# Experts' gate/up weights in half-chunk transfers, and a round's kind and units from registers

## What is computed

```python
logits = hf @ w_router + b_router               # 32 experts
top_vals, top_idx = lax.top_k(logits, 4)
weights = softmax(top_vals)
# each token's 4 experts:
gu = x_i @ w_gate_up[e] + b_gate_up[e]          # 1024 -> 2 x 1024
gate, up = split(gu); gate = min(gate, 7); up = clip(up, -7, 7)
act = (up + 1) * (gate * sigmoid(1.702 * gate))
y_i = act @ w_down[e] + b_down[e]               # 1024 -> 1024, weighted and summed per token
```

## Time and profile before

| | |
|---|---|
| median of three runs | 2881.35 us |
| profiled execution, its time | 2879.79 us |
| profiled execution, its span | 2877.9 us |
| TensorE (PE) busy | 2649.8 us, 92% |
| VectorE (DVE) busy | 1822.0 us, 63% |
| ScalarE (ACT) busy | 1468.4 us, 51% |
| GpSimd (POOL) busy | 353.7 us, 12% |
| bytes moved by DMA | 631 MB, 219 GB/s over the span |
| mean granted TensorE clock | 0.952 of full |

### The profile page before, as it was taken

How to read it: one execution, slowest core, us unless ns; L and a number is a source line. 1 busy time by engine, 2 the same in 40 slices (tenths; PEclk the granted TensorE clock), 3 DMA queues, 4 the chain that set the end, 5 groups by cost and what they waited for, 6 DMA issues and landing times. The chain is left out here.

```text
span 2877.9 us, 42547 instructions
## 1 busy us (share of the span) xinstructions
PE 2649.8 (92%) x12459; PEld 2139.7 (74%) x12460; DVE 1822.0 (63%) x2667; ACT 1468.4 (51%) x2138; POOL 353.7 (12%) x428
## 2 busy tenths in 40 slices
PE   4999799996799759999999999999999999999994
PEld 4888677775677648888888888888777777887771
DVE  5332144544555576566666665666699999999995
ACT  5221144442333245555555544555587777777771
POOL 0000011101001220111111111111111111111110
PEclk7999899997799769999999999999999999999995
DMA  6652222212334276666666666666699999999975
GB/s 238 240 200 82 98 81 70 70 41 91 106 123 163 96 260 239 216 214 215 213 217 213 217 224 216 225 225 219 221 361 366 360 370 363 364 363 365 367 270 189
DMA packets 188364, 631.14 MB, mean 219 GB/s; under 512 B 24931, under 2 KB 50709, under 8 KB 170245
## 3 DMA queue, kind: packets, MB, share of 16 engines
q1 hardware_dynamic: 162240, 554.07, 52.4%
q0 software_dynamic: 24832, 71.95, 9.8%
q10 hardware_dynamic: 1220, 4.21, 0.4%
HBM read 575.44 MB, written 64.73 MB: 222 GB/s over the span
## 5 line engine op out<-in xcount | busy, mean ns | idle before, releaser
L2535 DVE TENSOR_TENSOR e_gu_lo<-gu_raw,e_gu_hi 128x1024 fp32r<-128x1024 f32 x564 | 673.5, 1219 | 176.0 <-ACT e_gu_hi L2374 148.9
L83 PE MATMUL e_pgu<-e_gu_hi,e_x_hi 128*128 128x512 f32 x1568 | 638.9, 407 | 5.6 <-DVE e_x_lo L2565 5.6
L85 PE MATMUL e_pgu<-e_gu_hi,e_x_lo 128*128 128x512 f32 x1568 | 615.6, 393 | 0.0
L84 PE MATMUL e_pgu<-e_gu_lo,e_x_hi 128*128 128x512 f32 x1568 | 613.6, 391 | 0.0
L2374 ACT ACTIVATE e_gu_hi<-gu_raw 128x1024 fp32r<-128x1024 f32 x564 | 571.7, 1055 | 29.3 <-PEq L2766 19.9
L2541 DVE TENSOR_TENSOR e_dn_lo<-dn_raw,e_dn_hi 128x1024 fp32r<-128x1024 f32 x280 | 333.0, 1218 | 16.7 <-ACT e_dn_hi L2380 16.7
L85 PEld LDWEIGHTS e_pgu<-e_gu_hi,e_x_lo 128*128 128x128 f32 x1568 | 294.9, 188 | 64.3
L83 PEld LDWEIGHTS e_pgu<-e_gu_hi,e_x_hi 128*128 128x128 f32 x1568 | 296.0, 189 | 53.2 <-issue 5.9
L84 PEld LDWEIGHTS e_pgu<-e_gu_lo,e_x_hi 128*128 128x128 f32 x1568 | 296.4, 189 | 48.2
L83 PE MATMUL e_pdn<-e_dn_hi,e_a_hi 128*128 128x512 f32 x784 | 309.1, 394 | 22.3 <-DVE e_a_lo L2569 21.6
L85 PE MATMUL e_pdn<-e_dn_hi,e_a_lo 128*128 128x512 f32 x784 | 306.4, 391 | 0.0
(11 more groups left out here) (424 smaller groups left out, 3913.9 us busy)
## 6 DMA issues: line engine op xcount, KB each, us to landing
gu_raw<-in_w_gate_up_dram SPq DMA_DIRECT2D x560, 512.0 KB, 5.6
dn_raw<-in_w_down_dram SPq DMA_DIRECT2D x140, 1024.0 KB
wada_later<-in_w_ada_dram SPq DMA_DIRECT2D x32, 512.0 KB, 4.0
gu_bias<-hidden_bias SPq DMA_DIRECT2D x42, 256.0 KB, 10.8
win_raw<-in_w_in_dram POOLq DMA_DIRECT2D x5, 2048.0 KB
proj_by_token<-out_stage SPq DMA_DIRECT2D x32, 256.0 KB, 3.1
wg_raw<-in_w_in_dram POOLq DMA_DIRECT2D x16, 512.0 KB, 4.8
gates_transposed<-g_stage POOLq DMA_DIRECT2D x32, 256.0 KB, 2.3
```

What stands on the lines that cost most here:

```text
L83: pe.matmul(out, a[0], w[0], start=first, stop=False)
L84: pe.matmul(out, a[0], w[1], start=False, stop=False)
L85: return pe.matmul(out, a[1], w[0], start=False, stop=last)
L2535: dve.tensor_tensor(gu_lo[:, b, 2 * j:2 * j + 2], gu_raw[:, b, 2 * j:2 * j + 2].rearrange("p k g n -> p k (g n)"), gu_hi[:, b, 2 * j:2 * j ...
```

## The change

Gate/up weights are loaded in halves of a chunk: one DMA of 1 MB, for each partition one run of 8 KB; the layout in HBM is by half instead of by quarter. SP waits for the second piece of each half (`gu_lo_done` of pieces 2 and 4 of a chunk) before it issues a half. There are four landing semaphores for gate/up weights instead of eight, and ScalarE waits for one only at pieces 0 and 2. The pieces in which ScalarE and VectorE split remain quarters.

Two more values are kept in `m.rounds`: the unit at which the double rounds start (4 or 8) and a constant from which the units of single rounds count. In `rounds` each engine reads five values into registers ahead of the loop. In the loop the kind is a comparison of the round number with the register `both`, and U is a multiple of the loop register plus a register. No entry of the table is read in `rounds`; `expert_of`, SP's own loop and GpSimd's list address still read it.

```diff
--- before.py
+++ after.py
@@ -40,7 +40,6 @@
 LIST_WORDS = 3
 CH = 4
 FC = FF // CH
-QG = 4
 FIRST_K = 6
 TURN_A_K = 5
 GATE_MAX = LIMIT / (1.0 + math.exp(-ALPHA * LIMIT))
@@ -1887,8 +1886,8 @@
             for j in range(4):
                 sp.dma_start(braw[j * NE:(j + 1) * NE], m.b_gate_up[0, :, (j // 2) * FF:(j // 2 + 1) * FF]).then_inc(bias_raw, 16)
             for c in range(2):
-                for j in range(QG):
-                    load_gu(m, sp, 0, c, c, j, m.gu_in[c][j])
+                for half in range(2):
+                    load_gu(m, sp, 0, c, c, half, m.gu_in[c][half])
                 load_dn(m, sp, 0, c, c, m.dn_in[c])
             sp.wait_ge(bias_up, 1)
             for j in range(2):
@@ -2000,6 +1999,8 @@
                 v.inc(dve.tensor_copy(m.table[:, :, j], row2[:, j]))
             v.inc(dve.tensor_copy(m.rounds[:, 0:1], n_rounds[0:1]))
             v.inc(dve.tensor_scalar(m.rounds[:, 1:2], n_rounds[0:1], -1.0, None, ALU.add))
+            v.inc(dve.tensor_scalar(m.rounds[:, 3:4], one_ahead[0:1], -4.0, 8.0, ALU.mult, ALU.add))
+            v.inc(dve.tensor_scalar(m.rounds[:, 4:5], n_doubles[0:1], 4.0, 4.0, ALU.mult, ALU.add))
             v.step(dve.tensor_copy(m.rounds[:, 2:3], both_ahead[0:1]))
             keep_weights(dve, m, r, LAST, 0)
             dve.wait_ge(bias_hi, 1)
@@ -2018,10 +2019,10 @@
                             bounds_check=SEQ - 1, oob_is_err=False).then_inc(m.gathered[s], 16)
 
 
-def load_gu(m, sp, e, c, b, j, done):
-
-    k = slice(j * (KT // QG), (j + 1) * (KT // QG))
-    src = m.w_gate_up[0][bass.ds(e, 1), c, j].rearrange("a p k g n -> p (a k g n)")
+def load_gu(m, sp, e, c, b, half, done):
+
+    k = slice(half * (KT // 2), (half + 1) * (KT // 2))
+    src = m.w_gate_up[0][bass.ds(e, 1), c, half].rearrange("a p k g n -> p (a k g n)")
     sp.dma_start(m.gu_raw[:, b, k].rearrange("p k g n -> p (k g n)"), src).then_inc(done, 16)
 
 
@@ -2038,6 +2039,7 @@
 def phase_experts(nc, m):
     sem, sb = m.sem, m.scoped
     KD = FC // P
+    QG = 4
     with ExitStack() as ctx:
         gu_raw, dn_raw, bias, pick = m.gu_raw, m.dn_raw, m.gu_bias, m.pick
         gu_hi = sb(ctx, "e_gu_hi", [P, 2, KT, 2 * FC], F32R)
@@ -2100,20 +2102,23 @@
 
         def rounds(eng, body):
 
-            n = eng.value_load(m.rounds[0:1, 0:1], min_val=2, max_val=MAX_ROUNDS)
-            with eng.If(entry(eng, 0, 2, 1) > 0):
+            def count(j, least, top):
+                return eng.value_load(m.rounds[0:1, j:j + 1], min_val=least, max_val=top)
+
+            n, later, both = count(0, 2, MAX_ROUNDS), count(1, 1, MAX_ROUNDS - 1), count(2, 1, MAX_ROUNDS)
+            doubles_from, singles_from = count(3, 4, 8), count(4, 4, 4 * MAX_ROUNDS)
+            with eng.If(doubles_from > 4):
                 body(0, 0, True, True)
             with eng.Else():
                 body(0, 0, False, True)
-            with eng.Fori(1, n) as r:
-                U = eng.snap(entry(eng, r, 3, 4 * (MAX_ROUNDS * SLOTS)))
-                two = entry(eng, r, 2, 1)
-                with eng.If(two > 0):
-                    body(r, U, True, False)
+            with eng.Fori(0, later) as behind:
+                r = eng.snap(behind + 1)
+                with eng.If(r < both):
+                    body(r, eng.snap(8 * behind + doubles_from), True, False)
                 with eng.Else():
-                    body(r, U, False, False)
-
-            return eng.snap(entry(eng, n - 1, 3, 4 * (MAX_ROUNDS * SLOTS)) + 4 + 4 * entry(eng, n - 1, 2, 1)), n
+                    body(r, eng.snap(4 * behind + singles_from), False, False)
+
+            return eng.snap(4 * later + singles_from), n
 
         def units(two):
 
@@ -2132,8 +2137,8 @@
 
         @block.sync
         def _(sp):
-            def gu(e, c, b, j):
-                load_gu(m, sp, e, c, b, j, gu_in[b][j])
+            def gu(e, c, b, half):
+                load_gu(m, sp, e, c, b, half, gu_in[b][half])
 
             def dn(e, c, b):
                 load_dn(m, sp, e, c, b, dn_in[b])
@@ -2144,9 +2149,9 @@
 
             for b in range(2):
                 sp.sem_inc(bias_in[b], 16)
-            for j in range(QG):
-                wait_apart(sp, gu_lo_done, j + 1)
-                gu(0, 2, 0, j)
+            for half in range(2):
+                wait_apart(sp, gu_lo_done, (half + 1) * QG // 2)
+                gu(0, 2, 0, half)
 
             def body(r, U, two, final=False):
                 here = expert_of(sp, r)
@@ -2159,12 +2164,12 @@
                         wait_apart(sp, with_bias, U + 2 * c + 2)
                         bs(here, c + 1, (c + 1) % 2)
 
-                    for j in range(QG):
-                        wait_apart(sp, gu_lo_done, QG * q4 + QG * (c + 1) + j + 1)
+                    for half in range(2):
+                        wait_apart(sp, gu_lo_done, QG * q4 + QG * (c + 1) + (half + 1) * QG // 2)
                         if c == 0 or not final:
-                            gu(here if c == 0 else there, (c + 3) % CH, (c + 1) % 2, j)
+                            gu(here if c == 0 else there, (c + 3) % CH, (c + 1) % 2, half)
                         else:
-                            sp.sem_inc(gu_in[(c + 1) % 2][j], 16)
+                            sp.sem_inc(gu_in[(c + 1) % 2][half], 16)
 
                     wait_apart(sp, dn_lo_done, KD * q4 + KD * (c + 1))
                     if c < 2 or not final:
@@ -2197,9 +2202,9 @@
             for t in range(2):
                 sp.dma_start(m.c_x2[:, t], m.x2[t * P:(t + 1) * P, :]).then_inc(once_in, 16)
             wait_apart(sp, once_in, 64)
-            for j in range(QG):
-                wait_apart(sp, gu_in[0][j], 32 * n + 32)
-                wait_apart(sp, gu_in[1][j], 32 * n + 16)
+            for half in range(2):
+                wait_apart(sp, gu_in[0][half], 32 * n + 32)
+                wait_apart(sp, gu_in[1][half], 32 * n + 16)
             for b in range(2):
                 wait_apart(sp, dn_in[b], 32 * n + 16)
             wait_apart(sp, bias_in[0], 16 * n + 16)
@@ -2370,7 +2375,8 @@
             def gu_piece(r, c, j):
 
                 b = c % 2
-                act.wait_ge(gu_in[b][j], 32 * r + 16 * (c // 2) + 16)
+                if j % 2 == 0:
+                    act.wait_ge(gu_in[b][j // 2], 32 * r + 16 * (c // 2) + 16)
                 act.activation(gu_hi[:, b, 2 * j:2 * j + 2], gu_raw[:, b, 2 * j:2 * j + 2].rearrange("p k g n -> p k (g n)"), ACT.Copy).then_inc(gu_hi_done, 1)
 
             def dn_piece(r, c, j):
@@ -2776,7 +2782,7 @@
         m.csil = sb("silu_c", [P, KT], F32)
         m.wcT = sb("weights_transposed", [NE, NT, P], F32)
         m.table = sb("rounds", [1, MAX_ROUNDS + 2, 4], I32)
-        m.rounds = sb("round_count", [1, 3], I32)
+        m.rounds = sb("round_count", [1, 5], I32)
 
         vectors = ExitStack()
 
@@ -2833,11 +2839,11 @@
             m.pick = m.scoped(raw, "picked_rows", [P, 2, P], F32R)
             m.xg = m.scoped(raw, "e_xg", [P, SLOTS, D], F32)
             m.rows = m.scoped(raw, "e_rows", [P, SLOTS, LIST_WORDS], I32)
-            kept = [nc.alloc_semaphore(f"e_kept{i}") for i in range(14)]
-            m.gu_in = [kept[0:QG], kept[QG:2 * QG]]
-            m.dn_in = kept[8:10]
-            m.gathered = kept[10:10 + SLOTS]
-            m.rows_in, m.scattered = kept[12:14]
+            kept = [nc.alloc_semaphore(f"e_kept{i}") for i in range(10)]
+            m.gu_in = [kept[0:2], kept[2:4]]
+            m.dn_in = kept[4:6]
+            m.gathered = kept[6:6 + SLOTS]
+            m.rows_in, m.scattered = kept[8:10]
             phase_route(nc, m)
             end_phase()
             phase_sems.extend(kept)
@@ -2858,7 +2864,7 @@
 def laid_out(name, a):
 
     if name == "w_gate_up":
-        a = a.reshape(1, NE, QG, KT // QG, P, 2, CH, FC).transpose(0, 1, 6, 2, 4, 3, 5, 7)
+        a = a.reshape(1, NE, 2, KT // 2, P, 2, CH, FC).transpose(0, 1, 6, 2, 4, 3, 5, 7)
     if name == "w_down":
         a = a.reshape(1, NE, CH, FC // P, P, D).transpose(0, 1, 2, 4, 3, 5)
     return a
```

## The result

The changed kernel took 2857.65 us as the median of four runs (2856.02 to 2860.59), beside 2883.51 us for the kernel before in the same comparison; the ratio is 0.9909, 95% interval 0.9894 to 0.9924. Set beside each other again in a later comparison it was 2858.1 to 2880.45 us, ratio 0.9928 (0.9915 to 0.9941). It is thus 0.6 to 1.1% faster, some 22 us by the second comparison. The profiled executions differ by 2877.9 - 2856.4 = 21.5 us. In all kernels of this study executions fall 0 to 7 us apart by how long the phases ahead of the experts take (the first gate/up product starts anywhere from 1048 to 1056 us), so I read the stages of the expert phase, not totals, where a microsecond matters.

The account below looks back on a forecast made before the run. TensorE was taken as the bound in double rounds, with border holes in single rounds; -16.2 - 0.7 + 0.5 + 3.4 = -13.0 us gave 2866.8 us profiled, 2868 as median, 8-in-10 range 2858 to 2883.

Parts of the forecast that it names:

- the border of a round: Single stage: without two table loads, TensorE's 1.02 us hole shrinks by 0.85 in 19 rounds, -16.2 us.
- The arithmetic added: Round border: sum, register comparison and multiply-add replacing the loads cost 0.05 to 0.3 us, taken as 0.2.
- the whole hole: Single-stage borders: upper bound of the gain, 19 x 1.02 = 19.4 us, as TensorE is then full.
- Longer packets: Double stage: 8 KB runs delay the landing of slot 1's scatter, so TensorE loses 3.4 us more.
- raising all 13 by 0.5: Double stage: each of 13 scatter landings 0.5 us later; what exceeds 10.93 us costs 3.4 us more.
- Between the stages: Border from double to single rounds: the same two loads go, -0.7 us (0 to -0.83).
- The start: Start of the expert phase: three more register reads per engine, VectorE passes on 0.6; +0.5 us, bounds 0 and +1.5.
- The end: End of the expert phase: last round's entries not read again, TensorE still at its last down product; 0.
- The regrouping in time: Gate/up loads issued later in halves, up to about 3.7 us; over 6 us are left, so 0.
- The packets: Rival, double stage: scatter waits behind doubled runs; gains eaten at +1.5 us per landing, 2894 at +2.5; chance 0.17.
- DMA as the bound: Rival, single stage: cannot outrun the loads; at 368 GB/s the gain falls to 6.7, time 2878 us; chance 0.12.
- The borders shrank: Opposes the rival that round borders don't shrink, new arithmetic or another wait replacing the loads: 2881 to 2885 us; chance 0.09.

Follow-up runs that it names:

- registers, quarters: Changed kernel's registers in place of table reads, with the 512 KB quarter loads of the kernel before: 2860.0 us to 2880.45, ratio 0.9934.
- less work: Register kernels without the down product's third part (high weights by low activations); first executions 2737.11 us with quarter loads, 2746.66 with 1 MB halves.

## Why the prediction was wrong

Direction and mechanism were right; the time missed the range by 0.35 us on the fast side, and the size was short by two fifths: -13.0 us forecast, -21.5 between the profiled executions. Two terms carry the miss, the border of a round (-16.2 forecast) and the packets (+3.4 forecast); some 1.2 us more is the granted clock in the kernel before, for which the sum had no term.

**The border of a round, -16.2 us forecast.** The holes closed whole: a round went from 36.74 to 35.69 us (registers, quarters) where I had 0.85 us less, 19 x 0.20 = 3.8 us. The step that failed is the price of both sides of the exchange. The arithmetic added, "0.05 to 0.3 us; I take 0.2", was too dear. The rows show one fused operation of 41 ns and a branch of 45, and they run while the activation ahead is still busy, so of 0.99 us of idle time nothing remained. I had noted the end of that activation as a limit, and then let the arithmetic begin behind it. What VectorE gives back, 0.9 us, was too cheap: I took ScalarE's arithmetic for it, but from its first load at 2253.6 us to its branch it took 1.3 us:

```profile
L2111 DVEq COMPARE_BRANCH  x1: 56/56/56, 2254.9 to 2254.9; - x1
```

The bound of 19.4 us that I named as the whole hole was the better value: 19 rounds at 1.05 us are 20.0, and with 1.2 us for the clock and less 0.7 for one late round of the changed kernel (36.4 us instead of 35.7) that is the 20.6 measured.

**Longer packets, +3.4 us forecast.** The double stage became shorter instead: 1.8 to 2.3 us by the ruler, of which 1.1 is the ruler's error; from TensorE's hole at 1092.37 us (1093.00 after) to its last product ahead of the border between the stages it is 0.8 us. The step that failed is "raising all 13 by 0.5". ScalarE's waits for the scatter in the double stage, before and after:

```profile
ACT e_y L2418 <- DMA expert_sum<-e_y,e_dest: 2.7, 5, 0.9
```

```profile
ACT e_y L2424 <- DMA expert_sum<-e_y,e_dest: 2.0, 7, 0.4
```

With the halves more rounds wait, but by less. The landings became more even and stopped just where TensorE would begin to lose: in none of the five profiles with halves and the whole work does TensorE wait for `e_y` in the double stage. With quarters it does in seven of eight, in 1 to 11 rounds, which cost 0.6 to 7.3 us: about 1.2 us before, nothing with registers on all engines, 7.3 with registers on ScalarE and VectorE only. So in the profiles the halves took away up to 1.2 us where I had added 3.4; the times (ratio 0.9996) are too coarse to confirm it.

I had taken 13 landings of one execution as the kernel's own. That was not the mistake: the three kernels that were profiled twice repeat their double stage within 1.2 us. What moves the landings from kernel to kernel stays open. One rival is untested: in the six profiles with quarters in which GpSimd still reads at least one entry of the table at each border, the mean from slot 1's scatter to the next `e_y` is 11.05 to 11.56 us, in the two in which it takes the registers 10.68 and 10.79. No run changes GpSimd's reads alone.

**The smaller terms.** Between the stages the hole shrank by 1.01 us (0.7 forecast). The start cost 0.8 us by the first product of the phase, with a further wait of 0.23 us at the first `e_pat`. The size of 0.5 was near, but the path was wrong: I had "TensorE's are read while it waits for `e_x_lo`" and charged VectorE. VectorE starts this split at 1047.19 us, before at 1047.28, so it is not late. TensorE's own sequencer is. Its first branch and the wait behind it, before and after:

```profile
L2104 PEldq COMPARE_BRANCH  x1: 3505/3505/3505, 1040.4 to 1040.4; - x1
...
L2344 PEldq EVENT_SEMAPHORE  x1: 4015/4015/4015, 1044.0 to 1044.0; - x1
```

```profile
L2110 PEldq COMPARE_BRANCH  x1: 6444/6444/6444, 1042.3 to 1042.3; - x1
...
L2349 PEldq EVENT_SEMAPHORE  x1: 51/51/51, 1048.8 to 1048.8; - x1
```

Before, it stood 4.0 us at the wait. After, the five reads bring the branch 1.9 us later and the branch takes 2.9 us more, so nothing is left to wait for and the product starts when the sequencer comes. With registers and quarters the branch takes 4.96 us and the start costs nothing; why its duration differs stays open. The end cost 0.2 us (0 forecast). The regrouping in time, forecast at 0, is 0 in this kernel; the changed one has four waits for a down load, 3.8 us, in the single stage, and loses 0.4 us in one TensorE hole there; its second execution has 0.6 us of such waits and no hole.

**The rivals.** The packets did not decide. The 0.7 us at GpSimd agrees with the rule on packets that the prediction took from the Trainium skill (DMA: Bandwidth & Descriptors, "Queues, rings and completion order"); in the 6 to 8 us of the double stage with less work the length of the runs has little share or none. DMA as the bound fell: 374 GB/s in this kernel and 390 to 394 with less work, all at a share of 0.99 or more. The borders shrank. Of the floor of about 600 ns for a `tensor_load` in the Trainium skill (DMA: Bandwidth & Descriptors, "Latency and other measured facts"): the rows have 0.27 to 0.30 us, and one read with its arithmetic costs 0.49 us of a round (36.18 - 35.69), so the Trainium skill's figure is too high here, though the sum that I made with it, the whole hole, came out.

## What to carry to other kernels

A stretch without work at the top of a loop, named "issue" or a wait for a neighbour that has the same stretch, can be sequencer time, as here; count the register loads in it. If the time of several engines is that close, remove it on all of them at once, since each alone showed nothing here. Arithmetic on registers can run beside the instruction ahead of it, here two operations of 41 and 45 ns beside an activation of 0.62 us: price it from the start of that instruction, not from its end. And look at the reserve of every engine whose stream you lengthen, TensorE's too: what the loop saved was paid for in part by reads ahead of it.

## What was unexpected

The DMA share is no measure of what is left. It read 0.99 at 364 GB/s in the kernel before and 0.96 at 363 with halves and table reads, 0.99 at 374, and 1.01 to 1.02 at 390 to 394. And a releaser's name in a wait can be the second of two: with VectorE's own reads gone, 14 of 17 waits were still put down to "issue".
